# Two feed-forward weight halves begun on the first 128 tokens, and four conditioning sums moved in front of the output projection

## The reference, cut to what matters

```
x = x + concat([out_a, out_b, out_m]) @ w_out[l]                   # the output projection
x = x + conv_ffn(rms_norm(x, ffn_norm_g[l]), w_up[l], conv_w[l], conv_b[l], w_down[l])

def conv_ffn(h, w_up, conv_w, conv_b, w_down):
    u = h @ w_up                                                   # 256 x 1024 by 1024 x 5632
    up_pad = pad(u, 2 rows of zeros in front)
    uc = conv_b + sum(conv_w[i] * up_pad[:, i:i + s] for i in range(3))
    gate, val = split(uc, 2)
    return (silu(gate) * val) @ w_down

mod = silu(c) @ w_ada[l] + b_ada[l]                                # second block
sh1, sc1, g1, sh2, sc2, g2 = split(mod, 6)
```

## Time and profile before

| | |
|---|---|
| median of 3 runs | 1104.92 us (1104.28 to 1106.15) |
| the profiled execution's own time | 1109.6 us |
| its span (first to last instruction) | 1107.7 us |
| mean granted clock of PE in it | 0.926 of full |
| PE busy | 928.0 us, 84% of the span |
| PEld, DVE, ACT, POOL busy | 64%, 49%, 31%, 6% |
| DMA | 314.66 MB, mean 284 GB/s |

### The profile page before, as it was taken

How to read it: one execution, slowest core, us unless ns; L and a number is a source line. 1 busy time by engine, 2 the same in 40 slices (tenths; PEclk the granted TensorE clock), 3 DMA queues, 4 the chain that set the end, 5 groups by cost and what they waited for, 6 DMA issues and landing times.

```text
span 1107.7 us, 19063 instructions
## 1 busy us (share of the span) xinstructions
PE 928.0 (84%) x8322; PEld 713.3 (64%) x8322; DVE 542.3 (49%) x1004; ACT 347.4 (31%) x678; POOL 62.1 (6%) x81
## 2 busy tenths in 40 slices
PE   5998999999999999999999998657757665667665
PEld 4786777579999887988888975333424333334332
DVE  3446678756888856788765843221211121211121
ACT  3421144236767634544553341010101000000001
POOL 3102711000000000000000000000000000000000
PEclk9898999989999999999998999897879787988888
DMA  9442484474463565664548699999999999999994
GB/s 331 130 150 82 152 304 142 159 230 155 156 215 116 200 225 213 229 201 141 172 153 326 249 364 390 427 431 428 427 430 428 429 427 431 427 429 428 429 430 180
DMA packets 75065, 314.66 MB, mean 284 GB/s; under 512 B 3471, under 2 KB 27312, under 8 KB 62432
## 3 DMA queue, kind: packets, MB, share of 16 engines
q1 hardware_dynamic: 71236, 302.30, 69.3%
q0 software_dynamic: 3600, 11.04, 3.3%
q10 hardware_dynamic: 140, 0.04, 0.0%
HBM read 312.31 MB, written 1.06 MB: 283 GB/s over the span
## 4 chain that ended last, share of the span: by engine, by line
PE 59%; DMA 29%; DVE 6%; ACT 3%; issue 2%; POOL 2%; SPq 0%; DVEq 0%; ACTq 0%
PE ps L468 57%; DMA w<-in_w_up 21%; DMA w<-in_w_gate 3%; DMA w<-in_w_down 2%; DMA w<-in_w_ada 2%; DMA w<-in_w_in 1%; DVE sp L1794 1%; POOL w L840 1%; POOL w L843 1%; PE ps L2597 0%; PE ps L553 0%; PE ps L2044 0%; ACT sp L1785 0%; ACT hts L2692 0%; PE ps L978 0%
## 5 line engine op out<-in xcount | busy, mean ns | idle before, releaser
L468 PE MATMUL ps<-w,xg 128*32 128x256 f32 x2048 | 160.6, 478 | 106.7 <-DMA w<-in_w_up 83.3
L468 PE MATMUL ps<-hb,sp 128*128 128x256 f32 x1824 | 230.0, 286 | 0.0
L468 PEld LDWEIGHTS ps<-hb,sp 128*128 128x128 f32 x1824 | 221.6, 190 | 6.9 <-issue 6.2
L468 PEld LDWEIGHTS ps<-w,xg 128*32 128x32 f32 x2048 | 86.6, 132 | 179.2 <-issue 156.2
L1794 DVE TENSOR_TENSOR sp<-w,sp 128x1024 fp32r<-128x1024 f32 x122 | 144.7, 1219 | 42.8 <-ACT sp L1785 42.7
L1785 ACT ACTIVATE sp<-w 128x1024 fp32r<-128x1024 f32 x122 | 122.1, 1051 | 48.8 <-PE ps L468 48.8
L2756 DVE TENSOR_TENSOR cst<-ps,cst 64x256 f32<-64x256 f32 x32 | 13.7, 428 | 227.9 <-ACT cst L2688 227.9
L2688 ACT ACTIVATE cst<-ps 64x256 f32<-64x256 f32 x32 | 12.1, 377 | 328.5 <-PE ps L468 328.5
L2771 DVE TENSOR_TENSOR ost<-ps,cst 32x256 f32<-32x256 f32 x120 | 50.4, 420 | 100.2 <-PE ps L468 97.4
L468 PE MATMUL ps<-w,hts 128*32 128x256 f32 x1024 | 62.1, 382 | 13.6 <-ACT hts L2692 11.4
L468 PE MATMUL ps<-ht,w 128*128 128x256 f32 x256 | 63.8, 409 | 2.0 <-DMA w<-in_w_in 1.9
(11 more groups left out here) (399 smaller groups left out, 1148.5 us busy)
## 6 DMA issues: line engine op xcount, KB each, us to landing
w<-in_w_down SPq DMA_DIRECT2D x36, 2048.0 KB, 35.9
w<-in_w_gate SPq DMA_DIRECT2D x32, 2048.0 KB, 28.4
w<-in_w_up SPq DMA_DIRECT2D x32, 2048.0 KB, 32.8
w<-in_w_in SPq DMA_DIRECT2D x14, 2048.0 KB, 8.6
w<-in_w_up SPq DMA_DIRECT2D x22, 1024.0 KB, 7.6
w<-in_w_ada SPq DMA_DIRECT2D x8, 2048.0 KB, 9.5
w<-in_w_out SPq DMA_DIRECT2D x4, 2048.0 KB, 8.6
w<-in_w_ada POOLq DMA_DIRECT2D x8, 768.0 KB, 5.0
```

The lines of the kernel that those rows point to most:

```text
L468: return q.eng.matmul(o, l, r, start=start, stop=stop, skip_group_check=True)
```

## The change

It has three parts. The sums of chunks 0 to 3 go to the end of `beside_pe`, in front of `wout_pe(0)`, and into bank 6 (`mods_ve` and `adapair_pe` follow them there). Halves 0 and 1 of `w_up` are each multiplied in two steps: `up_first_pe` does the tokens of h = 0 right behind the output projection, and `up_pe` does those of h = 1 in its first two rounds. The moving operand of these matmuls is 128 columns wide, and there are twice as many. The junk of the second norm goes to SBUF (`xn1`), because it would fall on the banks 4 and 5, which now hold results.

```diff
@@ beside_pe
                 adasum_pe(q, i, take(q, i - 2))
                 free[i - 2] = [(s["ada"], i - 3)]
                 yield
+            take(q, 6)
+            for i in range(4):
+                adasum_pe(q, i, psum[6][:, 4 * i:4 * i + 4])
             yield
             yield from wout_pe(q, 0)
@@ up
+        hp_of = [[p[:, :, 128 * h:128 * h + 128] for p in hp] for h in range(2)]
+
+        def up_first_pe(q, j, ns):
+            q.wait_ge(s["nlo"], 2)
+            q.wait_ge(s["split"], 2 * j + 2)
+            b = take(q, UBANK[j])
+            for n in ns:
+                proj3(q, b[:, 256 * n:256 * n + 128], half_w(j), 128 * n, hp_of[0], 8)
+
         def up_pe(q):
             q.wait_ge(s["nlo"], 4)
             for j in range(22):
                 q.wait_ge(s["split"], 2 * j + 2)
-                b = take(q, UBANK[j])
-                for h in range(2):
-                    t = proj3(q, b[:, 256 * h:256 * h + 256], half_w(j), 128 * h, hp, 8)
+                b = psum[UBANK[j]] if j < 2 else take(q, UBANK[j])
+                for n in range(2):
+                    if j < 2:
+                        t = proj3(q, b[:, 256 * n + 128:256 * n + 256], half_w(j), 128 * n, hp_of[1], 8)
+                    else:
+                        t = proj3(q, b[:, 256 * n:256 * n + 256], half_w(j), 128 * n, hp, 8)
                 t.then_inc(s["half_mm"], 1)
@@ mods_ve: both reads
-psum[7][:, 0:16]     psum[7][:, 16:24]
+psum[6][:, 0:16]     psum[6][:, 16:24]
@@ scalar
-            norm_sc(q, 2, x, rdy2, psum_all[:, 2048:3072], (1,))
+            norm_sc(q, 2, x, rdy2, xn1[:, 1024:2048], (1,))
@@ tensor
-            take(q, 7)
-            for i in range(4):
-                adasum_pe(q, i, psum[7][:, 4 * i:4 * i + 4])
+            up_first_pe(q, 0, (0, 1))
+            up_first_pe(q, 1, (0,))
             feat_pe(q, 2, xn1, ft2, hs=(1,))
-            adapair_pe(q, 6, psum[7][:, 16:24])
-            free[7] = [(s["ada"], 4)]
+            up_first_pe(q, 1, (1,))
+            adapair_pe(q, 6, psum[6][:, 16:24])
+            free[6] = [(s["ada"], 4)]
             up_pe(q)
```

More of the change, by code:

```diff
@@ L1945, in mods_ve @@
             q.wait_ge(s["ada_sum"], 7)
-            q.eng.tensor_tensor(modc[:, 0:16], psum[7][:, 0:16], col("b_ada_2", 0, 16), ADD).then_inc(s["ada"], 1)
+            q.eng.tensor_tensor(modc[:, 0:16], psum[6][:, 0:16], col("b_ada_2", 0, 16), ADD).then_inc(s["ada"], 1)
             q.wait_ge(s["par2"], N_PAR2)
-            q.eng.tensor_tensor(modc[:, 16:24], psum[7][:, 16:24], pk[:, 8:16], ADD).then_inc(s["ada"], 1)
+            q.eng.tensor_tensor(modc[:, 16:24], psum[6][:, 16:24], pk[:, 8:16], ADD).then_inc(s["ada"], 1)
             q.wait_ge(s["ada"], 3)
```

## The result

| | before | changed |
|---|---|---|
| median | 1105.49 us (5 runs, 1104.28 to 1108.91) | 1125.14 us (5 runs, 1124.01 to 1131.74) |
| ratio, 95% interval | | 1.0188 [1.0163, 1.0212] |
| profiled execution, its span | 1109.6, 1107.7 us | 1124.49, 1122.6 us |

The kernel is 19.7 us slower, where +7.4 was forecast and 1106 to 1118 was the range. The direction was right and the size was not.

A forecast was written before the change was run, and what follows sets the result against it. The prediction took PE to bound the stretch of the change. Its terms, +9.8 for short matmuls, -3.3 for the vanished clock fall and +0.9 for one at the projection, made +7.4 us: median 1104.9 to 1112.3, range 1106 to 1118.

The forecast's parts named there:

- step 1: Halves 0 and 1 on PE: 192 short matmuls at 110.6 ns replace 96 at 119.1 ns, +9.8 us.
- A (59.6): Rival on halves 0 and 1: short matmuls cheap at 59.6 ns, 1102.5 us; chance 0.06, half way 0.05.
- B (231): Rival on halves 0 and 1: short form loses the float32r rate, 231 ns a matmul, 1135.5 us; chance 0.08.
- steps 4 to 6: Waits on the new path, later users of the halves, and the second norm's junk in SBUF: 0 us each.
- rival D: The delay is swallowed by the DMA stage behind the change, 1105 to 1107 us; chance 0.03.
- step 2: PE's half-clock fall from 240.9 to 247.7 us goes and no fall is expected there, -3.3 us.
- if PE's clock falls in them: Sign that the forecast is wrong: PE's clock falls in the short matmuls, expected at 1.00 from 240 to 262.
- rival C: The 192 short matmuls are too light, so the clock falls there: +10.7 us, 1115.6; all at half speed 21 more; chance 0.05.
- step 3: Sums of chunks 0 to 3 before the output projection: a half chance of a clock fall losing 1.7 us, +0.9 us.

The follow-up runs named there:

- E4: Kernel before, order kept, with the sums of chunks 0 to 3 and the pair sum given 128 moving columns instead of one: 0.9952, 1102.94 us.
- E7: Kernel before with only halves 8 to 11 of w_up, mid feed-forward, multiplied in 128-column matmuls (384 in place of 192): 1.0176, 1124.7 us.
- E5: Changed kernel with only the 8 matmuls of the pair sum made 128 columns wide: 1.0095, 1117.13 us.
- E2: Changed kernel with the pair sum and its reader on DVE moved behind the second step of half 1: 1.0089, 1117.55 us.
- E6: Kernel before, order kept, with halves 0 and 1 multiplied in 128-column matmuls (192 in place of 96): 1.0255, 1136.23 us.
- E8: Changed kernel with the one-column sums of chunks 0 to 3 put back behind the output projection: 1.0263, 1136.5 us.
- E3: Kernel before with only the sums of chunks 0 to 3 moved in front of the output projection: 1.0052, about +5.8 us.
- E1: Changed kernel with the sums of chunks 0 to 3 and the pair sum given 128 moving columns instead of one: 1.0043, 1111.92 us.

## Why the prediction was wrong

**The work (step 1) was right.** The short matmul costs what its 128-column weight load costs: 32 float32 records take 3.54 us with one moving column and 3.57 with 128 (E4), and PEld was busy for all 43 us of E7's short stream. I took 110.6 ns from the one-column sums; E7 measured 111.5, and the changed kernel 113 to 117 at full clock. Rivals A (59.6) and B (231) are out. The 81 ns of the Trainium skill (page "TensorE: Matmul & The Clock Gate", section "Back-to-back issue gap") does not hold for these float32r pairs: 111.5 measured. The early halves cost 10 us of PE's time and fill nothing.

**The waits (steps 4 to 6) were right.** None of PE's rows in the stretch has idle time, and the shift reached the first expert load in full, so rival D is out.

**The clock at the old place (step 2): its first half was right.** The fall at 241 to 248 did go, worth 3.4 us. The sentence that failed is "I expect no fall here". I reasoned that the pair sum alone, 1.8 us with "full-width matmuls on both sides", could not tip the clock. It did: made wide (E5) no fall follows it, with one column a fall follows in the middle of the stream (changed) and behind it (E2). That it was put at 0 cost +10.2 us, and the prediction had named the sign: "if PE's clock falls in them". The neighbours were also misread: they are not full but the short float32r matmuls that the change itself makes. A pair sum with full matmuls on both sides was not run, so whether the short ones in front help to tip the clock stays open; what those behind do is shown next. The trace of the kernel before held a warning (timeline and windows as above):

```profile
588.63 1.95 PE L468 MATMUL ps<-cst,w 128*128 128x1 f32 x16
592.40:599.20 6.80, 6.80 (x28) 5.96 (x27) 4.21 (x12) 1.62 (x4) 0.57 (x1) 0.50 1.03 381
```

These are 16 one-column records again, far from the change, between matmuls of 256 moving columns (those next to them fill only part of the array: 128*16, 128*32 and 16*128, and PE idles for 0.28 us in between). A fall begins 1.9 us after them, and in each of the ten traces one does, 0.8 to 3.9 us after them, for 3.4 or 6.8 us. The one-column records are not shown to be its cause, but they speak against "no fall here".

**The length of a fall was taken from the wrong row.** All my prices for a fall, in step 2 and in rival C, came from rows in which 256- or 512-column matmuls ended it after 3.4 to 6.8 us. Under short matmuls it did not end: 20.5 us here, the whole stream in E6 and E8. Rival C had the right place, and the 10.2 us lie below its upper price (21 us for all 192), but its cause was not the right one: the stream alone does not lose the clock (E7). I gave it 0.05, on the strength of a stretch at 182.8 to 187.0 that kept its clock. That row shows that narrow matmuls can keep a clock they have, which E7 confirms; it says nothing on whether they win it back. Those are two questions, and I asked one.

**The clock at the front (step 3) was sized too small.** I gave a fall a half and 1.7 us, so +0.9. It was there in the changed kernel and in E2, E3 and E5, all that have one-column sums at that place, for 6.8 us in each, 3.4 lost, the upper end of what I had allowed. With wide sums (E1) the clock is at 1.00 from 206. So the terms of the forecast that failed are both of the clock: +10.2 where I had 0, and +3.4 where I had +0.9.

The Trainium skill, page "TensorE: Matmul & The Clock Gate", section "HAM oscillation — how this bites in real kernels", tells of the clock as lost in gaps in which PE idles. These traces differ: PE has no idle time between 199 us and the fall at 252.6, nor in that fall, nor in the 44 us of E6. Its clock fell while it was busy, with one-column sums just before. Why these sums tip it, the runs don't say. Loads of the weights went at the same pace with one column and with 128, and only the former were followed by a fall here; no experiment tried a width between.

## What to carry to other kernels

Before a wait is filled with split matmuls, compare a full matmul with its own stationary load: here 119 ns against 111, so halving the moving columns nearly doubled the work (192 x 111.5 ns for 96 x 119.1). Look at the granted clock on both sides of every one-column reduction on TensorE. Where the stationary load bounds it anyway, give it a wide moving operand (128 columns here); E4, the kernel before with wide sums, was 0.5% faster (0.2 to 0.7), and in the changed kernel 8 wide matmuls took away half of the slowdown (E5). And price a lost clock by what follows it: the short stream kept a clock that it had and did not win back one that was lost.

## What the runs showed that was not expected

- A stream of narrow float32r matmuls (128 moving columns, PE always busy) kept the full clock for 43 us (E7, 111.5 ns apart), and stayed at half of it for its whole 41 us when the clock had fallen before (E6, 214 ns apart). In these runs it left neither state.
- The same 16 one-column records were followed by 20.5 us at half speed ahead of 96 short matmuls and by 3.4 us ahead of full ones (E2).
- 32 float32 records with one moving column take 3.54 us and with 128 columns 3.57 us (E4).
